# Expert stage of a hybrid MoE block: the eighth sum moves to the gate/up bank, the look-up to the third sum's bank, and whole token tiles are summed before half ones

## The reference, cut to what matters

```python
scores = sigmoid(xt @ router_w); idx = top_k(scores + router_bias, 6)     # 64 experts
wts = s_sel / sum(s_sel) * 2.5
y = sum over the 6 chosen e:  w_e * ((silu(x @ we_gate[e]) * (x @ we_up[e])) @ we_down[e])   # 1024 -> 256 -> 1024
y = y + shared_swiglu(x)
h = layer_norm(ALPHA * h + y)
```

## Time and profile before

| | |
|---|---|
| three runs, median | 1192.36 us |
| profiled execution, its own time | 1194.98 us |
| its span | 1193.1 us |
| instructions | 18993 |
| PE busy | 1134.5 us, 95% |
| DVE busy | 732.6 us, 61% |
| ACT busy | 443.0 us, 37% |
| POOL busy | 208.4 us, 17% |
| moved by DMA | 285.85 MB, mean 240 GB/s |

### The profile page before, as it was taken

How to read it: one execution, slowest core, us unless ns; L and a number is a source line. 1 busy time by engine, 2 the same in 40 slices (tenths; PEclk the granted TensorE clock), 3 DMA queues, 4 the chain that set the end, 5 groups by cost and what they waited for, 6 DMA issues and landing times.

```text
span 1193.1 us, 18993 instructions
## 1 busy us (share of the span) xinstructions
PE 1134.5 (95%) x6912; PEld 695.3 (58%) x6912; DVE 732.6 (61%) x1268; ACT 443.0 (37%) x692; POOL 208.4 (17%) x116
## 2 busy tenths in 40 slices
PE   5999999999999999999999999999999999999993
PEld 4889798888888888646534434444444344444441
DVE  8848485858585867764644455555544555555447
ACT  7656565666565657302002212221122122211224
POOL 1423333424242424101010000000000000000000
PEclk9989999999999999999999999999999999999997
DMA  6121212122130303149089999999999999999921
GB/s 232 48 99 41 106 42 103 60 85 91 55 116 29 124 21 141 36 158 399 34 339 419 417 417 417 417 417 415 415 418 412 417 413 412 419 418 417 402 90 70
DMA packets 48295, 285.85 MB, mean 240 GB/s; under 512 B 9088, under 2 KB 10624, under 8 KB 16528
## 3 DMA queue, kind: packets, MB, share of 16 engines
q1 hardware_dynamic: 43088, 272.96, 56.4%
q0 software_dynamic: 5184, 12.59, 2.8%
HBM read 287.62 MB, written 4.19 MB: 245 GB/s over the span
## 4 chain that ended last, share of the span: by engine, by line
PE 47%; DVE 6%; issue 2%; DMA 1%; ACT 1%; DVEq 0%; POOLq 0%
PE pair L1376 21%; PE pair L1413 10%; PE pair L1403 5%; DVE acc L1501 4%; PE pair L885 3%; PE pair L170 2%; PE pair L1044 1%; PE pair L1387 1%; DMA xg<-h_rows,idx 1%; PE pair L1037 1%; DVE acc L1559 0%; ACT first L1478 0%; DVE table L1268 0%; PE pair L1031 0%; PE pair L852 0%
## 5 line engine op out<-in xcount | busy, mean ns | idle before, releaser
L376 PE MATMUL pair<-hT,w_parts 128*128 128x264 f32 (+1 forms) x2112 | 381.1, 340 | 1.7 <-DVE hT L636 1.3
L376 PEld LDWEIGHTS pair<-hT,w_parts 128*128 128x128 f32 x2112 | 323.9, 191 | 48.8 <-issue 4.8
L223 POOL TENSOR_TENSOR w_parts<-w_raw,w_parts 128x1024 fp32r<-128x1024 f32 x66 | 165.9, 2514 | 314.0 <-ACT w_parts L217 302.9
L1501 DVE TENSOR_TENSOR acc<-acc,pair 128x512 f32<-128x512 f32 x280 | 170.6, 682 | 39.6 <-PE pair L1403 39.6
L1376 PE MATMUL pair<-raw,xgT 128*64 128x512 f32 x768 | 170.1, 595 | 0.0
L877 POOL DMA_INDIRECT xg<-h_rows,idx x36 | 35.8, 993 | 546.4 <-DVE idx L871 546.4
L1461 ACT ACTIVATE y_hi<-pair,small 128x512 fp32r<-128x512 f32 x70 | 48.1, 687 | 214.8 <-PE pair L1413 214.8
L1376 PEld LDWEIGHTS pair<-raw,xgT 128*64 128x64 f32 x768 | 53.0, 137 | 116.0 <-issue 116.0
L1492 DVE TENSOR_TENSOR act_a<-act_s,pair 128x256 f32<-128x256 f32 x35 | 14.8, 422 | 170.2 <-ACT act_s L1454 170.2
L1403 PE MATMUL pair<-y_hi,ST 64*128 64x512 f32 (+1 forms) x280 | 83.2, 448 | 14.9 <-DVE acc L1501 13.4
L1454 ACT ACTIVATE act_s<-pair 128x256 f32<-128x256 f32 x35 | 13.4, 383 | 224.3 <-PE pair L1376 224.3
(11 more groups left out here) (289 smaller groups left out, 1287.0 us busy)
## 6 DMA issues: line engine op xcount, KB each, us to landing
raw<-in_w_gate_up SPq DMA_DIRECT2D x96, 1024.0 KB
raw<-in_w_down SPq DMA_DIRECT2D x48, 1024.0 KB
first<-in_w_gate_up SPq DMA_DIRECT2D x44, 1024.0 KB
w_raw<-in_w_in SPq DMA_DIRECT2D x36, 1024.0 KB, 6.7
first<-in_w_down SPq DMA_DIRECT2D x22, 1024.0 KB
xin<-in_x SPq DMA_DIRECT2D x4, 512.0 KB, 5.5
ws_gu<-in_ws_gate_up SPq DMA_DIRECT2D x1, 2048.0 KB, 7.8
h_rows<-acc SPq DMA_DIRECT2D x4, 512.0 KB, 21.1
```

Source lines behind the costliest of these rows:

```text
L223: pool.tensor_tensor(w[:, n % PARTS, 1], w_raw[:, n // 2, n % 2], w[:, n % PARTS, 0].bitcast(F32), ALU.subtract).then_inc(sem("w_lo_ready" ...
L376: last = pe.matmul(o, w[:, n % PARTS, pw, k * P:(k + 1) * P], hT[ph][:, k, of], start=(k == 0 and m == 0), stop=(k == KB - 1 and m == 2))
L1501: v.tensor_tensor(part, part, SUM[g], ALU.add).then_inc(sem("sum_free"), 1)
```

## The change

It does five things.

- The eighth sum goes to bank 0 (gate/up and `AT`), the look-up to bank 6, that of the third sum. The first three look-ups, made ahead of the stage, stay in bank 0.
- `SUMS` and `TILES` put the two tiles of all slots first.
- `scatter` no longer waits for the third sum to be added. It waits ahead of its second group for the previous look-up to have been read, and ahead of its last for ACT's copy `aT`.
- `one` waits before `look_up` for three sums to be added (which covers the wait before `down` for two).
- `gate_up` waits for the eight sums to be added instead of for the look-up to be read; the wait before `turn_x` goes.

```diff
-        self.SUM = tuple(banks[n] for n in (4, 5, 6, 7, 1, 2, 3, 6))
+        self.SUM = tuple(banks[n] for n in (4, 5, 6, 7, 1, 2, 3, 0))
+        self.LOOK = banks[6]
...
-    def look_up(self, pe, p, b, item):
+    def look_up(self, pe, p, b, item, to=None):
+        to = self.LOOK if to is None else to
         pe.wait_ge(self.sem("S_built"), 2 * p + 2)
...
-            last = pe.matmul(self.GU[:, 0:PAIR * TAB], ...
+            last = pe.matmul(to[:, 0:PAIR * TAB], ...
...
-    SUMS = ((0, 0, LOW), (TT - 1, 0, HIGH), (0, 1, LOW), (TT - 1, 1, HIGH)) + \
-        tuple((t, m, slice(0, P)) for t in range(1, TT - 1) for m in range(2))
-    TILES = (0, TT - 1, 1, 2)
-    SHARED, AGAIN = 4, 2
+    SUMS = tuple((t, m, slice(0, P)) for t in range(1, TT - 1) for m in range(2)) + \
+        ((0, 0, LOW), (TT - 1, 0, HIGH), (0, 1, LOW), (TT - 1, 1, HIGH))
+    TILES = (1, 2, 0, TT - 1)
+    SHARED, LAST = 4, ADDS - 2
+    LOOK_AT = 2
...
-        def gate_up(p, b, turn):
-            pe.wait_ge(sem("look_free"), p + 3)
+        def gate_up(p, b, turn, first=False):
+            if not first:
+                pe.wait_ge(sem("sum_free"), ADDS * p)
...
                 if g == SHARED and next_x:
                     pe.wait_ge(sem("xgT_ready"), 2 * p + 4)
-                if g == ADDS - 2:
-                    pe.wait_ge(sem("sum_free"), ADDS * p + AGAIN + 1)
+                if g == LOOK_AT:
+                    pe.wait_ge(sem("look_free"), p + 3)
+                if g == LAST and next_x:
+                    pe.wait_ge(sem("aT_ready"), p + 1)
...
             scatter(p, (b + 2) % THIRDS)
-            pe.wait_ge(sem("aT_ready"), p + 1)
+            pe.wait_ge(sem("sum_free"), ADDS * p + LOOK_AT + 1)
             pairs.look_up(pe, p + 3, b, item)
-            pe.wait_ge(sem("sum_free"), ADDS * p + 2)
             down(p, b, turn)
...
-            act.wait_ge(sem("sum_free"), ADDS * (THIRDS * n_rounds + 2) + (3, 4, 6, 8)[t])
+            act.wait_ge(sem("sum_free"), ADDS * (THIRDS * n_rounds + 2) + (2, 4, 7, 8)[t])
...
             add_one(last, g)
-            if g == 5:
+            if g == 3:
                 mean(0)
```

More of the change, by code:

```diff
@@ L846, in build, with looked_up @@
                             at.broadcast_to([P, TT, PAIR, HALF]), ALU.is_equal).then_inc(self.sem("S_built"), 1)
-    def look_up(self, pe, p, b, item):
+    def look_up(self, pe, p, b, item, to=None):
+        to = self.LOOK if to is None else to
         pe.wait_ge(self.sem("S_built"), 2 * p + 2)
         for t in range(TT):
-            last = pe.matmul(self.GU[:, 0:PAIR * TAB], self.Sb[b][:, t].rearrange("p h u s -> p (h u s)"),
+            last = pe.matmul(to[:, 0:PAIR * TAB], self.Sb[b][:, t].rearrange("p h u s -> p (h u s)"),
                              self.mem["table"][:, bass.ds(item, PAIR), t], start=(t == 0), stop=(t == TT - 1))
         last.then_inc(self.sem("look_done"), 1)
-    def looked_up(self, v, p, b, first=False):
-        sem, GU = self.sem, self.GU
+    def looked_up(self, v, p, b, first=False, at=None):
+        sem, at = self.sem, self.LOOK if at is None else at
         v.wait_ge(sem("look_done"), p + 1)
@@ L860, in looked_up @@
             v.wait_ge(sem("look_free"), p)
-        v.tensor_tensor(self.looked, GU[:, 0:PAIR * TAB].rearrange("p (u n) -> p u n", u=PAIR), self.of_item,
+        v.tensor_tensor(self.looked, at[:, 0:PAIR * TAB].rearrange("p (u n) -> p u n", u=PAIR), self.of_item,
                         ALU.mult).then_inc(sem("look_step"), 1)
@@ L1113, in _ @@
         pe.wait_ge(sem("table_ready"), 1)
-        pairs.look_up(pe, 0, 0, 0)
+        pairs.look_up(pe, 0, 0, 0, pairs.GU)
         pe.wait_ge(sem("a_shared_ready"), 2)
@@ L1117, in _ @@
         pe.wait_ge(sem("look_free"), 1)
-        pairs.look_up(pe, 1, 1, PAIR)
+        pairs.look_up(pe, 1, 1, PAIR, pairs.GU)
         shared_down(1)
         pe.wait_ge(sem("look_free"), 2)
-        pairs.look_up(pe, 2, 2, 2 * PAIR)
+        pairs.look_up(pe, 2, 2, 2 * PAIR, pairs.GU)
         shared_down(2)
@@ L1280, in _ @@
         for b in range(THIRDS):
-            pairs.looked_up(v, b, b, b == 0)
+            pairs.looked_up(v, b, b, b == 0, pairs.GU)
         v.wait_ge(sem("h1_stored"), 16 * TT)
@@ L1416, in down @@
                 last.then_inc(sem("y_done"), 1)
-        gate_up(0, 0, 0)
+        pe.wait_ge(sem("look_free"), THIRDS)
+        gate_up(0, 0, 0, True)
         pairs.turn_x(pe, 1, 16)
@@ L1422, in _ @@
         pe.wait_ge(sem("aT_ready"), 1)
+        pe.wait_ge(sem("shared_taken"), TT)
         pairs.look_up(pe, 3, 0, 3 * PAIR)
-        pe.wait_ge(sem("shared_taken"), TT)
         down(0, 0, 0)
```

## The result

The changed kernel takes 1184.07 us, the median of 11 runs (1183.07 to 1189.02), the kernel before 1193.2 us in its 11 (1189.37 to 1196.1): ratio 0.9931, 95% interval 0.9915 to 0.9948, that is 0.7% or 8 us faster (9.1 us by the two medians). The forecast was 1190.2 with 1182 to 1196: the time is in the range, but it is the time of the first rival (1183.4), and the likeliest case, "within 0.5%", did not come. The profiled execution took 1183.69 us, with a span of 1181.8.

What follows compares the result with a forecast made beforehand. The prediction took PE as the bound, with one stall per iteration; 34 iterations x 0.08 us gave 2.7 gained, less 0.5 at the end, 2.2 us off the 1192.36 median: 1190.2 us, range 1182 to 1196.

Steps and rivals of the forecast that it cites:

- the first rival: Before the look-up: register work does not come last, PE's path holds, 0.28 us an iteration gained, 1183.4 us; chance 0.24.
- the likeliest case: Whole kernel: a gain of 0 to 5 us, 1187.5 to 1192 us, chance 0.50; within 0.5% had 0.66.
- PE is the bound, with one stall an iteration: Expert stage: PE sets the 15.90 us iteration, stalling 0.47 us before scatter's last group for DVE's third sum.
- What is late next: register work behind the third add: Between third add and down: the look-up's address operations lose their cover, down 0.68 us after the wait clears.
- A satisfied wait still costs 0.20 us: Scatter's group borders: a weight load carrying an already met wait adds 0.20 us to the matmul steps.
- The two rules turned down: Two skill rules not granted: weight loads pulled ahead make the new wait free; the sequencer queues waiting instructions and goes on.
- PE's path: Scatter to down: 0.47 us of stall less one more wait at 0.20, so 0.28 us shorter.
- the sign that the prediction gave for this rival: Changed trace: an iteration of 15.62 us would show register work off the path; 15.82 was expected.
- the sequencer step: Before the look-up: the sequencer stands behind the wait for the third sum, so register work starts only at 815.58.
- The lead of the loads: Expert stage: loads end some 10 us or more ahead of PE's need, so they do not bind.
- The end, 0.5 us lost: After the last pair: four adds instead of two remain behind mean, a loss of about 0.5 us, once.

Runs made afterwards that it cites:

- e_banks_only: The changed kernel with the old order of sums (half tiles first) kept, so only banks and waits change: 1177.35 us, ratio 0.9868 to the kernel before.
- e_regs_behind: The changed kernel with four more long-met waits against registers between the wait for the third sum and the look-up: 1183.97 us, ratio 0.993.
- e_look_mid: The changed kernel with the look-up moved between the two halves of down: 1174.78 us, ratio 0.9852 to the kernel before.
- e_static_address: The changed kernel with every look-up in the loop reading one fixed place, without the four address operations (computation partly replaced): 1174.95 us, ratio 0.9852.

## Why the prediction was right or wrong

- **PE is the bound, with one stall an iteration; it goes; nothing waits for the loads.** Right: the idle on DVE is gone, and no matmul of the stage waits for weights.
- **What is late next: register work behind the third add.** The mechanism is right, and so is its size: from L852 (L850 before) to down 0.7 us, 0.68 forecast. Taking the operations away gives 0.44 us an iteration back (15.64 to 15.20), four more cost 0.5, and hiding them under down gives 0.37. So this is what the change leaves unused.
- **"A satisfied wait still costs 0.20 us": the step that failed.** The prediction put 0.20 us on each border with a wait, and kept 812.40 as the start of scatter, 0.20 behind the last transpose. Both were the change between 128 and 64 rows. With whole tiles first the scatter starts 0.02 behind the transpose (806.91 to 806.93; e_banks_only, with half tiles first, 0.21: 807.92 to 808.13), and the groups, forecast at distances of 1.12, 1.12 and 0.66, come at 1.02, 1.01 and 0.57. The third add then clears at 3.16 after the transpose, not at 3.38 (815.58 - 812.20): 0.22 us earlier, most of it the earlier start. With 0.03 of register work the other way, the gain is 0.27 an iteration for 0.08, 9 us for 2.7.
- **The two rules turned down.** The Trainium skill ("TensorE: Matmul & The Clock Gate", part 1, on queue depths) has weight loads pulled ahead of matmuls in flight. That agrees with the trace at the border of two whole groups, wait or no wait (0.24 and 0.23 us from start to start); at a change between 128 and 64 rows the trace shows 0.20 us on top. The Trainium skill ("Perfetto Trace Analysis", tensor engine instruction) has the sequencer push an instruction with its wait into a queue and go on. Why L850 stood until 815.1 in the kernel before was not tested. After the change the wait is with the operation of L852, which stands until the add is done; in e_regs_behind the operations ahead of it ran 2 us early.
- **PE's path (the first rival).** Forecast 0.28 shorter, and 1183.4 is what came, by accident: the rival had the register work off the path, and it is on it. Where it is off, in pair 1 of the changed kernel, the gain is 0.77 an iteration (down at +3.37 for +4.14) and not 0.28. Two errors nearly cancel, and the iteration of 15.64 falls on the sign that the prediction gave for this rival (15.62), while the sequencer step that it was to refute holds. That the time lies in the range is in part luck: the likeliest case, 1187.5 to 1192, missed it.
- **The lead of the loads, "some 10 us or more".** Enough for this change; e_look_mid and e_static_address use it up at 17 to 18 us under before.
- **The end, 0.5 us lost.** Wrong, it cost nothing. I took the 0.46 between mean and the seventh add for DVE's own; the note at that row says that it waited for PE. After the change the adds follow at once, 0.10 behind mean (1163.81 to 1163.91).

The net account of the change: from the third add to down 1.23 us (the last group's 1.04 and the look-up's 0.19) became 0.71, 0.52 less; the first group whole instead of half, so the add 0.25 later. 0.52 - 0.25 = 0.27. The runs give both terms by themselves: banks and waits alone bring 15.90 down to 15.38 (0.52), and the new order on top of them costs 0.26.

## What to carry to other kernels

When a wait is moved, look at what the engine's sequencer computes behind it: register operations that lay under queued matmuls come onto the path at 0.13 us each, and the engine's busy rows hide it as a few tiny instructions that have grown apart. Put such a look-up where enough work is queued ahead of it. And before a gap between two instructions is put down to a wait, find a border of the same kind without the wait.

## What the runs showed of the hardware that was not expected

- A change between matmuls on 128 rows and on 64 costs 0.20 us: the two steps behind it take 0.66 us together, and 0.46 without a change. A wait already met costs nothing at a weight load (0.24 us from start to start with it, 0.23 without).
- A register operation of PE's sequencer is 0.046 us long in the profile, but four matmuls that each need one start 0.13 us apart, and the four together take 0.56 us for 0.26 without.
- The stage has a floor in its loads. When they bind, an iteration lasts 16.14 to 16.19 us, more than the 15.90 of before: the stage stays under it only as long as the lead lasts.
